# Re-sequencing the triple mixer of a fused transformer kernel

## What is computed

```python
h = rms_norm_2(x, mix_norm[l])
z = h @ w_in[l]
(na_q, na_k, na_v, gq, gk, gv, gr, gfl, gbl, c_q, c_kv, k_rope, gates) = split_cols_2(z, IN_SPLITS)
y_na = neighborhood_attention(rms(na_q), rms(na_k), na_v, na_rpb[l])            # 8 heads of 64
g_f = log_sigmoid(gfl @ gla_gf_up[l] + gla_gf_bias[l]) / 16                     # g_b likewise
o_gla = gla_bidirectional(gq, gk, gv, g_f, g_b)                                 # 4 heads, chunks of 64
y_gla = rms_norm_2(o_gla, gla_out_norm[l]) * silu(gr)
y_mla = mla_attention(c_q, c_kv, k_rope, ...)       # norm, up-projection, norm, rope, 4 heads of 192
gt = sigmoid(gates.reshape(B, S, N_BRANCH, D))
mixed = gt[0]*(y_na @ w_br_na) + gt[1]*(y_gla @ w_br_gla) + gt[2]*(y_mla @ w_br_mla)
x = x + mixed @ w_out[l]
```

## Time and profile before

| | us |
|---|---|
| median of 3 runs (lowest, highest) | 2682.18 (2680.72, 2685.68) |
| the profiled execution's own time | 2676.76 |
| its span, first to last instruction | 2675.0 |
| granted TensorE clock, mean over the span | 0.961 of full speed |
| TensorE busy in matmuls | 2505.0 |
| VectorE, ScalarE busy | 1848.3, 1144.3 |

### The profile page before, as it was taken

The page is one execution under the profiler, slowest core; times in us unless marked ns, Lnnn a source line. Parts: engine busy times, 40 slices in busy tenths (PEclk is TensorE's granted clock), DMA queues, the critical chain, the costliest instruction groups (busy, mean ns, idle before and its releaser), DMA issues.

```text
span 2675.0 us, 40045 instructions
## 1 busy us (share of the span) xinstructions
PE 2505.0 (94%) x16770; PEld 2265.9 (85%) x16770; DVE 1848.3 (69%) x2229; ACT 1144.3 (43%) x1265; POOL 67.6 (3%) x80
## 2 busy tenths in 40 slices
PE   6999999999999599999999987899999998888999
PEld 5999799998999478989999777789899997776898
DVE  6778646877777757778776546587777765465876
ACT  4335564434334343343345634433433456343432
POOL 0000000000000012000000000130000000000000
PEclk9999999999999699999999978999999998899999
DMA  5555336555555035555555223375555552242554
GB/s 163 189 188 161 108 127 192 182 184 176 185 187 169 32 96 173 189 173 189 188 164 183 91 71 126 90 203 187 175 177 186 170 182 95 75 141 70 170 187 141
DMA packets 307720, 410.08 MB, mean 153 GB/s; under 512 B 9446, under 2 KB 274124, under 8 KB 307580
## 3 DMA queue, kind: packets, MB, share of 16 engines
q1 hardware_dynamic: 304176, 400.61, 46.9%
q0 software_dynamic: 2672, 6.17, 1.4%
q10 hardware_dynamic: 732, 1.29, 0.2%
HBM read 407.00 MB, written 1.05 MB: 153 GB/s over the span
## 4 chain that ended last, share of the span: by engine, by line
PE 76%; DVE 11%; DMA 6%; ACT 5%; issue 2%; DVEq 0%; SPq 0%; ACTq 0%; PEldq 0%
PE bank L525 22%; PE acc L537 19%; PE bank L528 12%; PE bank L924 10%; PE acc L2027 2%; ACT part_hi L451 2%; DVE part_lo L458 2%; PE bank L920 2%; DMA raw<-in_w_in 2%; DMA raw<-in_ffn_w 1%; PE bank L1020 1%; DVE hT L737 1%; DMA raw<-in_ffn_w_up 1%; PE acc L525 1%; PE bank L1779 1%
## 5 line engine op out<-in xcount | busy, mean ns | idle before, releaser
L451 ACT ACTIVATE part_hi<-raw 128x2048 fp32r<-128x2048 f32 x383 | 728.0, 1905 | 995.5 <-DMA raw<-in_ffn_w 399.6
L458 DVE TENSOR_TENSOR part_lo<-raw,part_hi 128x2048 fp32r<-128x2048 f32 x383 | 874.3, 2286 | 308.6 <-ACT part_hi L451 306.8
L525 PE MATMUL bank<-hT,part_hi 128*128 128x512 f32 x2688 | 687.7, 396 | 23.8 <-DVE hT L737 21.3
L525 PEld LDWEIGHTS bank<-hT,part_hi 128*128 128x128 f32 x2688 | 485.9, 190 | 122.8 <-DVE hT L737 21.2
L537 PE MATMUL acc<-gated,part_hi 128*128 128x256 f32 x2816 | 522.9, 284 | 7.0 <-DVE squares L625 7.0
L537 PEld LDWEIGHTS acc<-gated,part_hi 128*128 128x128 f32 x2816 | 447.5, 193 | 7.4 <-issue 7.4
L924 PE MATMUL bank<-part_hi,hT 128*128 128x256 f32 (+1 forms) x2336 | 440.4, 289 | 6.4 <-DVE hT L737 4.6
L537 PE MATMUL acc<-gated,part_lo 128*128 128x256 f32 x1408 | 399.9, 284 | 0.0
L528 PEld LDWEIGHTS bank<-hT,part_lo 128*128 128x128 f32 x2688 | 369.8, 192 | 26.2
L924 PEld LDWEIGHTS bank<-part_hi,hT 128*128 128x128 f32 x2336 | 375.5, 196 | 14.7 <-issue 6.8
L528 PE MATMUL bank<-hT,part_lo 128*128 128x256 f32 x2688 | 377.6, 284 | 0.0
(11 more groups left out here) (388 smaller groups left out, 2296.9 us busy)
## 6 DMA issues: line engine op xcount, KB each, us to landing
raw<-in_ffn_w SPq DMA_DIRECT2D x132, 1024.0 KB, 5.3
raw<-in_w_in SPq DMA_DIRECT2D x52, 1024.0 KB, 5.2
raw<-in_ffn_w_gate SPq DMA_DIRECT2D x44, 1024.0 KB, 5.3
raw<-in_ffn_w_up SPq DMA_DIRECT2D x44, 1024.0 KB, 5.3
raw<-in_ffn_w_down SPq DMA_DIRECT2D x44, 1024.0 KB, 4.9
raw<-in_hy_w_in SPq DMA_DIRECT2D x22, 1024.0 KB, 5.2
raw<-in_hy_w_out SPq DMA_DIRECT2D x8, 1024.0 KB, 5.0
raw<-in_w_out SPq DMA_DIRECT2D x8, 1024.0 KB, 4.9
```

What stands on the lines that cost most here:

```text
L451: t.e.activation(part_hi[:, n % SLOTS, 0:size], raw[:, n % SLOTS, 0:size], ACT.Copy).then_inc(hi_ready, 1)
L458: t.e.tensor_tensor(part_lo[:, n % SLOTS, 0:size], raw[:, n % SLOTS, 0:size], part_hi[:, n % SLOTS, 0:size].bitcast(F32), ALU.subtract).th ...
L525: pe.matmul(b.rearrange("p (h s) -> p h s", h=2), slot_cols(s, 0)[:, k, f * P:(f + 1) * P], hT[:, :, k, :], start=(k == 0), stop=False, sk ...
```

## The change

Everything is in the triple mixer, but for six more small gain loads at the program's start.

1. MLA's preparation goes up between the `z` pieces: the `z` order changes, the two up-projection pieces come after the sixth `z` piece, `mla_scale` folds the query norm into the softmax, gains are applied where a transposed tile is copied, and the 64-wide rope parts are stored two heads to a tile.
2. NA's scores, flips and values use the `acc` banks, and the rotating banks hold GLA's low-rank gates, flips and cumulative sums, worked at steps 1, 2, 4, 5, 7 and 8; its gate pieces stand at steps 1, 3, 5 and 9.
3. GLA's updates stand between the two halves of NA's branch product; its chunk products, output and norm alternate with gate pieces; GLA's branch product is filler in MLA's first two attention steps, and four gate pieces fill the next four.
4. The gates are `tanh` of half the argument, with 0.5 folded in later (`combine` adds 1, the `mix` copies scale by 0.5), instead of a sigmoid.

```diff
-Z_TILES = (12, 13, 14, 10, 11, 0, 1, 2, 3, 4, 5, 6, 7, 8, 9)
+Z_TILES = (12, 13, 14, 0, 1, 2, 3, 10, 11, 4, 5, 6, 7, 8, 9)
...
+        def gate_scalar(t, n):
+            act = t.e
+            b = t.banks.take(by_piece=True)
+            next_hi(t)
+            if n in (4, 8):
+                act.wait_ge(gt_free, t.see(gt_free))
+            act.wait_ge(piece_done, through(t))
...
+                ins = act.activation(gt[:, a, c:c + COLS], halves(b)[:, a, :], ACT.Tanh, scale=root_half[:, a:a + 1])
...
+        def na_scalar(t, l):
...
+                if i == 4:
...
+                    act.wait_ge(gl_in, t.see(gl_in))
+                    t.link(act.activation(ge[:, :, :, :], ge[:, :, :, :], ACT.Exp))
+                    act.activation(ge[:, :, :, :], ge[:, :, :, :], ACT.Ln, bias=1.0).then_inc(gl_log, 1)
...
+        def na_vector(t, l):
...
+                if i in NA_GATES:
+                    project_vector(t, 1)
+                if i == 9:
+                    grow(t)
...
+            next_lo(t)
...
         def gla_tensor(t, l):
             pe = t.e
+            pe.wait_ge(gla_ke, t.see(gla_ke))
             for d in range(2):
...
-            pe.wait_ge(dve_operand, t.see(dve_operand))
+            branch_tensor(t, 2)
+            pe.wait_ge(gla_qk, t.see(gla_qk))
...
+            project_tensor(t, [COLS])
+            pe.wait_ge(gla_state, t.see(gla_state))
             for parity in range(2):
...
+            project_tensor(t, [COLS] * 2)
+            pe.wait_ge(go_ready, t.see(go_ready))
+            made = flip_banks(t, lambda k, a: go[:, a, k, :], 4)
             project_tensor(t, [COLS])
...
         def gla_vector(t, l):
             dve = t.e
+            updates = [t.banks.take() for _ in range(4)]
+            filled_to = [t.banks.filled[b] for b in updates]
+            next_lo(t)
             for d in range(2):
...
+        def mla_tensor(t, l, go_made):
...
+                if i in (0, 1):
+                    pe.wait_ge(*go_made[i])
+                    branch_tensor(t, 2 * i)
+                if 2 <= i <= 5:
+                    project_tensor(t, [COLS])
...
         def triple_tensor(t, l):
...
+            project_tensor(t, Z_W[6:10])
+            pe.wait_ge(mla_src, t.see(mla_src))
+            flip_banks(t, lambda h, a: lq[:, a, h * MLA_QK:h * MLA_QK + P], 4)
+            flip_banks(t, lambda h, a: lk[:, a, h, :], 4)
+            flip_banks(t, lambda k, a: qr[:, a, k * P:(k + 1) * P], 2)
+            flip_banks(t, lambda k, a: kr[:, a, k * P:(k + 1) * P], 2)
+            project_tensor(t, Z_W[10:12])
+            pe.wait_ge(na_src, t.see(na_src))
...
         def triple_scalar(t, l):
...
+            project(6, 7)
+            act.wait_ge(norm_src, t.see(norm_src))
+            act.activation(squares[:, 0:TT * MLA_H * MLA_QK], lq[:, :, :].rearrange("p a c -> p (a c)"), ACT.Square)
+            act.activation(k_squares, lk[:, :, :, :].rearrange("p a h d -> p (a h d)"), ACT.Square)
...
+            project(7, 8)
+            rms_scalar(t, head_views(z, Z_NK, NA_H, 64), TT * NA_H, 64)
+            project(8, 9)
...
+            act.activation(z[:, :, Z_GR:Z_GR + 512], z[:, :, Z_GR:Z_GR + 512], ACT.Silu).then_inc(gr_ready, 1)
+            project(9, 10)
...
         def triple_vector(t, l):
...
+            kv_made = evicted(t, b)
+            project_vector(t, 1)
...
+            dve.wait_ge(*kv_made)
+            dve.sem_inc(norm_src, 1)
...
+                              ky.to_broadcast([P, TT, MLA_H, 64]), ALU.mult).then_inc(mla_src, 1)
+            dve.wait_ge(mla_src, t.see(mla_src))
+            norm_heads(Z_NK, [k_made])
+            dve.sem_inc(na_src, 1)
+            project_vector(t, 2)
...
+                  A["mla_q_norm_2"][:, 0:P], A["mla_k_norm_2"][:, 0:P]):
...
+        for v in (A["na_q_norm_2"], A["na_k_norm_2"]):
+            for half in range(2):
+                small(gain_rows[at:at + DEPTH, 1, half * 64:(half + 1) * 64], v)
```

More of the change, by code:

```diff
@@ L2238, in gla_vector @@
-            for d in range(2):
-                of_half = [filled(t), filled(t)]
+                of_half = updates[2 * d:2 * d + 2]
+                for j in range(2):
+                    dve.wait_ge(full[of_half[j]], filled_to[2 * d + j])
                 for n in range(3):
@@ new lines, in triple_scalar @@
+            project(5, 6)
+            rms_scalar(t, head_views(z, Z_NQ, NA_H, 64), TT * NA_H, 64)
+            act.wait_ge(c_roots, t.see(c_roots))
+            for i, n in enumerate((3, 4)):
+                for c in range(n):
+                    if c == n - 1:
+                        b = t.banks.take(by_piece=True)
+                        next_hi(t)
+                        act.wait_ge(piece_done, through(t))
+                    else:
+                        b = filled(t)
+                    for a in range(TT):
+                        src, root = halves(b)[:, a, :], stat[:, 2, 24 + 2 * i + a:25 + 2 * i + a]
+                        if i == 0:
+                            ins = act.activation(lq[:, a, c * 256:(c + 1) * 256], src, ACT.Copy, scale=root)
+                        else:
+                            act.activation(lk[:, a, c, :], src[:, 0:P], ACT.Copy, scale=root)
+                            ins = act.activation(lv[:, a, c, :], src[:, P:2 * P], ACT.Copy, scale=root)
+                    ins.then_inc(taken[b], 1)
@@ L2394, in triple_scalar @@
+            t.banks.take()
+            project(10, 12)
+            flip_out(t, na_qT, 4, gain[:, G_NQ + l:G_NQ + l + 1], P, 0)
+            flip_out(t, na_kT, 4, gain[:, G_NK + l:G_NK + l + 1], P, 0)
+            project(12, 15)
             na_scalar(t, l)
@@ L2396, in triple_scalar, with c_gain @@
             mla_scalar(t, l)
-            split_flip_scalar(t, hT, KD)
-            next_hi(t)
+            for k0 in range(0, KD, 2):
+                b = filled(t)
+                act.activation(hT[:, 0, k0:k0 + 2, :], halves(b), ACT.Copy, scale=0.5).then_inc(flip_hi, 1)
             down_scalar(t, KD, to_x=True)
+        def c_gain(l, k):
+            at = (G_CQ if k < 2 else G_CKV) + 2 * l + k % 2
+            return gain[:, at:at + 1]
         def triple_vector(t, l):
+            dve = t.e
@@ new lines, in triple_vector @@
+            t.link(ins)
+            norm_heads(Z_NQ, [evicted(t, (t.banks.next - 1) % 4)])
+            for n in (3, 4):
+                for c in range(n):
+                    b = t.banks.take(by_piece=(c == n - 1))
+                next_lo(t)
+            kv_made = evicted(t, b)
+            project_vector(t, 1)
+            k_made = evicted(t, (t.banks.next - 1) % 4)
+            dve.wait_ge(*kv_made)
+            dve.sem_inc(norm_src, 1)
+            t.see(norm_src)
+            dve.wait_ge(squares_ready, t.see(squares_ready))
@@ L2415, in triple_vector @@
+            flip_out(t, lkT, 4, gain[:, G_MK + l:G_MK + l + 1], P, 1)
+            t.banks.take()
+            b = filled(t)
+            dve.tensor_copy(lkrT[:, :, :], halves(b)).then_inc(taken[b], 1)
+            project_vector(t, 2)
+            flip_out(t, na_qT, 4, gain[:, G_NQ + l:G_NQ + l + 1], P, 1)
+            flip_out(t, na_kT, 4, gain[:, G_NK + l:G_NK + l + 1], P, 1)
+            project_vector(t, 3)
             t.see(root_row_ready)
-            t.e.wait_ge(to_dve, t.see(to_dve))
@@ L2420, in triple_vector @@
             mla_vector(t, l)
[L2421 to L2422 removed]
+            for k0 in range(0, KD, 2):
+                b = filled(t)
+                dve.wait_ge(flip_hi, t.see(flip_hi))
+                dve.scalar_tensor_tensor(hT[:, 1, k0:k0 + 2, :], halves(b), 0.5, hT[:, 0, k0:k0 + 2, :].bitcast(F32),
+                                         ALU.mult, ALU.subtract).then_inc(taken[b], 1)
             down_vector(t, KD)
```

882 lines of the change are left out of this document (501 added, 381 removed).

## The result

The changed kernel is faster, by half of what was forecast. That is 28 to 29 us won, where the sum said 58.7. The first timing lies 32 us above the predicted 2623.5 and 6 above the upper end of the range, 2650; the second lies at that end, beside a kernel before that was 5 us faster as well.

The account below looks back on a forecast made before the run. TensorE bounds the kernel, each mixer losing 64.9 us to idle time and slow clock. Loss falls to 35.2, with 1.0 less work: 30.7 per mixer, twice 61.4, less 2.7 is 58.7; median 2623.5 us, range 2596 to 2650.

Parts of the forecast that it names:

- The work: MLA's rope halves, keys and queries: transposed two at a time, eight transpositions instead of sixteen, 1.0 us less per mixer.
- The wait among the `z` pieces: Before MLA's transposition inside `z`: 10.4 us of TensorE idle per mixer, plus 1.0 at the up-projection's start.
- The rival that it would be hidden: Among the `z` pieces: a shorter VectorE chain hides the wait, 10.4 + 1.0 us per mixer go, 2601; chance 0.2.
- NA: NA with GLA woven in: waits of 0.7 us at its flips and 7.5 in its steps, 2.2 of that at the tail.
- The output: GLA's output: leaves the low clock behind a gate piece, saving 7.1 us, with 2.9 after it, 10.0 in all.
- the rival that doubted it: GLA's output stays at 0.50, 7.1 us per mixer, 2638; with NA's waits doubled, 2653; chance 0.28.
- The 2.3 us for the split before the updates: GLA: one `next_lo` stands before the new updates and stalls 2.3 us.
- MLA and the end: MLA's attention: 0.5 us of stall, small attention waits 2.0 and 1.7; end: 1.8 before `mix` is transposed, 0.3 more.
- Slow clock: Remaining low clock behind TensorE's waits in each mixer: 7 us, from 1.5 per wait over 1 us before.
- the signs set down with the prediction: `z` wait about 10 us, GLA's output near 1.00, MLA's transpositions waiting under 1 us, idle near 28 us per mixer.
- Outside the mixers: Program start: six more gain loads in ScalarE's queue put the end off by at most 2.7 us.
- Cost at nothing: ScalarE's table loads: tanh leaves 3 per mixer against 14, saving 14 us of ScalarE, counted as no gain.

Follow-up runs that it names:

- f3_keynorm: Changed kernel with NA's key norm moved in ScalarE's and VectorE's queues to behind the copies of MLA's transposed tiles: 2634.96 us, ratio 0.9844 to the kernel before.
- after_again: The changed kernel, unedited, timed and profiled once more: 2649.55 us, ratio 0.9894 to the kernel before.
- f1_end: Changed kernel with VectorE's last combination moved ahead of the split of w_out's second piece: 2631.8 us, ratio 0.9832 to the kernel before.
- f12347: Changed kernel with four reorderings (mixer end, GLA updates, NA key norm, NA tail) and spread bias loads together: 2585.00 us, ratio 0.9653 to the kernel before.
- f7_spread: Changed kernel with the second mixer's 16 bias loads issued one per weight piece instead of all at once: 2640.05 us, ratio 0.9841 to the kernel before.
- before_again: The kernel before the change, unedited, run once more for its profile: 2678.56 us.
- tanh_before: Kernel before with only tanh in place of the sigmoid in the mixer's gate pieces: 2674.30 us, ratio 0.9977 to the kernel before.
- sigmoid: Changed kernel with the gates' sigmoid and its factors put back: 2655.92 us, ratio 0.9911 to the kernel before.

## Why the prediction was wrong

**What bounds the kernel.** Right. TensorE's idle time and its low clock were the two things to win, 64.9 us per mixer (63.6 and 63.5 between the ends used here), and 47.5 and 49.1 are left of it, where the sum left 35.2.

**The work.** Forecast 1.0 us less per mixer; measured 3.3 (267.5 to 264.2 us at full clock, summed over the trace). Where the other 2.3 come from stays open.

**The wait among the `z` pieces.** Forecast 11.4 us idle, with ScalarE's queue as its last link; measured 8.6, from the same chain, ScalarE's blocked queue. VectorE's own preparation was ready 0.6 us late, not 2.5. The rival that it would be hidden did not come, and `f3_keynorm` shows that half of it need not be there.

**NA.** Forecast 0.7 + 5.3 in its flips and steps and 2.2 at the tail; measured 3.3 (1.9 in `after_again`) and 3.6. The place of the tail's wait was right, its cause was not named: `grow` in front of the last lo parts.

**GLA.** The output was forecast to leave the low clock, 14.20 us to about 7; it took 7.9 (1601.40 to 1609.29) at 1.00. This step, the surest gain of the change, was right, and the rival that doubted it wrong. The 2.3 us for the split before the updates became 4.6 and 3.9: the mechanism was named, the term was mis-sized, since VectorE had to wait 12.00 us for the load and the hi part of that split (until 1586.57).

**MLA and the end.** 4.2 us of small waits were forecast where 0.3 came. But the end, "1.8 before `mix` is transposed", was carried over from the old profile, and there the sum failed: the new order puts two splits ahead of the last combination, and the wait is 7.7. This is one line of the diff that I had read for its banks and not for its place in the queue. `f1_end` prices the fault at 16 us.

**The idle time as a whole** was forecast at 28.2 us per mixer (35.2 less the 7.0 of slow clock) and measured at 29.6 and 29.3. That it fits is luck: the `z` pieces, NA and MLA came out shorter than their terms and GLA's updates and the end longer, and the errors cancel.

**Slow clock.** The largest error. Forecast 7.0 us per mixer, measured 17.9 and 19.8. This term failed, and the signs set down with the prediction did not watch it: the output at 1.00, 0.6 us before MLA's transpositions and idle time near 28 us all came. I priced a wait at 1.5 us of slow clock, from a profile in which eight waits shared 12.1, and left out GLA's output, where one wait of 2.8 had 10.0 behind it. In the new profile five waits of 3 to 9 us (those among the `z` pieces counted as one) carry 18, some 3.6 each. A count of waits is thus no measure. In proportion to idle time the old mixer's 24.3 for 39.3 would have given 17 for the 28.2 forecast; but `f12347` has 3.4 for 13.8, and waits of 1.62 and 3.12 us were followed by 6.8 and by none at the low clock, so that is no rule either. What sets the clock's share stays open; what the runs show is that it went down with the waits, from 17.9 to 3.4 us per mixer in `f12347`.

**Outside the mixers.** Forecast 2.7 us, all at the start. Measured 1.2 at the start (1.8 in the second pair), 2 to 8 more in the lead, and 6.5 to 9.1 between the mixers, where I had not looked at all, although the change takes two loads out of POOL's queue there and `f7_spread` shows that this burst costs 14 us.

In sum, for the first pair of profiles: 58.7 forecast, less 23.8 in the mixers (the clock's 10.9 and 12.8, the rest as good as cancelled), 9.1 between them and 6.2 in the lead, is 19.6, and the spans differ by 19.2. For the second pair (`before_again`, `after_again`): less 20.0, 6.5 and 1.5, is 30.7, and they differ by 30.0. The timings say 28 to 29. None of the rivals was what happened. The second, from 2638 to 2653, comes near the measured time, but GLA's output did not stay at the low clock and NA's waits did not double.

**Tables.** "Cost at nothing" was 6 us out in the old order (`tanh_before`); in the new one `sigmoid` leaves open whether it is nothing or as much.

## What to carry to other kernels

Where each engine runs a queue that is written by hand, ask of every reordering what stands directly ahead of the instruction that TensorE will wait for: here a split of a weight piece, whose load cannot start before TensorE itself has moved on, stood ahead of it in two places, and moving two lines won as much as the whole change. Look for the slow clock behind every wait; here 29.6 us of idle time in a mixer went with 17.9 us of slow clock, though no single wait had a fixed price. And look at the bulk loads of the neighbouring stages: a burst of small loads next to a stream of weight loads cost 14 us here when it went out at once, and no wait over 0.7 us when it went out one load per weight piece.

## What the runs showed of the hardware

Beside a burst of 16 loads of 128 KB a 1 MB weight load took 21.3 us from its issue until ScalarE could use it, where one alone landed in 5.2, and put behind GLA the same burst led to a wait of 13.8 us; spread out, the same 2 MB made no wait over 0.7 us. The price of a wait in slow clock varied at one and the same place: 3.28 us of idle time was followed by 8.5 us at 0.50, 1.62 by 6.8, and 2.97 and 3.12 by none. Small transpositions without a wait ahead of them ran at 1.00. A table load delayed the next activation by 1.29 us.
